# RMS norms on one core: where the squares are added and how the root is spread back

## The reference, cut to what matters

```python
def rms_norm(x, w):
    xf = x.astype(F32)
    y = xf * lax.rsqrt(jnp.mean(xf * xf, -1, keepdims=True) + NORM_EPS) * w.astype(F32)
    return y.astype(x.dtype)

def block(x, mods, nw, fw_in, fw_out, mixer, params, init_state):
    sh1, sc1, g1, sh2, sc2, g2 = mods
    h = rms_norm(x, nw[0]) * (1 + sc1) + sh1
    out, state = mixer(h, init_state, *params)
    x = x + g1 * out
    h = rms_norm(x, nw[1]) * (1 + sc2) + sh2
    x = x + g2 * swiglu(h, fw_in, fw_out)
    return x, state
```

## Time and profile before

| what | value |
|---|---|
| runs of the kernel | 2957.46, 2961.81, 2971.84 us (median 2961.81) |
| the profiled execution: its time | 2957.81 us |
| the profiled execution: its span | 2956.0 us |
| mean granted TensorE clock | 0.903 of full speed |
| TensorE matmul / weight load busy | 2465.6 / 2249.1 us (83% / 76%) |
| VectorE / ScalarE busy | 1293.3 / 903.4 us (44% / 31%) |

### The profile page before, as it was taken

How to read it: one execution, slowest core, us unless ns; L and a number is a source line. 1 busy time by engine, 2 the same in 40 slices (tenths; PEclk the granted TensorE clock), 3 DMA queues, 4 the chain that set the end, 5 groups by cost and what they waited for, 6 DMA issues and landing times.

```text
span 2956.0 us, 51987 instructions
## 1 busy us (share of the span) xinstructions
PE 2465.6 (83%) x21424; PEld 2249.1 (76%) x21424; DVE 1293.3 (44%) x2212; ACT 903.4 (31%) x1697; POOL 0.2 (0%) x4
## 2 busy tenths in 40 slices
PE   4799579649996669999797699999985869999797
PEld 2799366238884459999797598888864869999796
DVE  1311644375565442222322477878874232221323
ACT  1322222213331132222212356555553132221311
POOL 0000000000000000000000000000000000000000
PEclk8899678569998789999899799999987989999898
DMA  5122424210001212222122133333330212222121
GB/s 199 50 72 77 142 72 171 92 32 7 3 3 58 78 40 67 76 73 76 52 70 96 39 100 98 94 98 97 93 111 22 64 36 71 78 71 76 54 70 49
DMA packets 319412, 216.46 MB, mean 73 GB/s; under 512 B 11640, under 2 KB 304902, under 8 KB 318854
## 3 DMA queue, kind: packets, MB, share of 16 engines
q1 hardware_dynamic: 260944, 179.66, 20.3%
q10 hardware_dynamic: 58294, 34.41, 3.9%
HBM read 205.74 MB, written 8.29 MB: 72 GB/s over the span
## 4 chain that ended last, share of the span: by engine, by line
PE 75%; DVE 18%; ACT 2%; issue 2%; DMA 1%; DVEq 1%; ACTq 1%; SPq 0%
PE bank L271 46%; PE bank L2022 10%; PE bank L494 2%; PE bank L1279 2%; DVE wide_low L289 1%; PE bank L2057 1%; DVE arena L1492 1%; ACT arena L487 1%; PE bank L412 1%; PE bank L1364 1%; PE bank L2061 1%; DMA ring<-in_mod_w_dram 1%; DVE ring_low L2111 1%; DVE rstd L505 1%; PE bank L1382 1%
## 5 line engine op out<-in xcount | busy, mean ns | idle before, releaser
L271 PE MATMUL bank<-narrow_high,w_split 128*128 128x320 f32 x4096 | 774.0, 311 | 80.9 <-DVE w_split L279 80.9
L271 PEld LDWEIGHTS bank<-narrow_high,w_split 128*128 128x128 f32 x4096 | 648.1, 189 | 81.9 <-issue 81.9
L279 DVE TENSOR_TENSOR w_split<-ring,w_split 128x1024 fp32r<-128x1024 f32 (+1 forms) x192 | 229.4, 1202 | 597.3 <-ACT w_split L276 588.4
L271 PE MATMUL bank<-narrow_low,w_split 128*128 128x320 f32 x2048 | 469.7, 311 | 0.0
L271 PE MATMUL bank<-wide_high,w_split 128*128 128x320 f32 x1920 | 371.3, 316 | 85.5 <-DVE w_split L279 85.5
L276 ACT ACTIVATE w_split<-ring 128x1024 fp32r<-128x1024 f32 (+1 forms) x192 | 198.9, 1042 | 754.5 <-PE bank L271 408.7
L271 PEld LDWEIGHTS bank<-wide_high,w_split 128*128 128x128 f32 x1920 | 310.5, 193 | 87.5 <-issue 87.5
L271 PEld LDWEIGHTS bank<-narrow_low,w_split 128*128 128x128 f32 x2048 | 345.7, 189 | 0.0
L271 PE MATMUL bank<-wide_low,w_split 128*128 128x320 f32 x960 | 223.9, 315 | 0.0
L2022 PE MATMUL bank<-x_high,pair_high 128*128 128x320 f32 x768 | 186.7, 325 | 30.0 <-DVE ring_low L2111 29.9
L1679 DVE TENSOR_TENSOR arena<-arena,bank 128x640 f32 (+1 forms) x44 | 36.1, 821 | 366.8 <-PE bank L271 366.8
(11 more groups left out here) (353 smaller groups left out, 2994.6 us busy)
## 6 DMA issues: line engine op xcount, KB each, us to landing
ring<-in_mod_w_dram SPq DMA_DIRECT2D x96, 512.0 KB, 4.7
ring<-in_ffn_w_in_dram SPq DMA_DIRECT2D x88, 512.0 KB, 3.8
ring<-in_od_w_in_dram SPq DMA_DIRECT2D x48, 512.0 KB, 4.1
arena<-cumulative_decays ACTq DMA_DIRECT2D x80, 256.0 KB, 3.5
ring<-in_ev_w_in_dram SPq DMA_DIRECT2D x32, 512.0 KB, 3.8
ring<-in_ffn_w_out_dram SPq DMA_DIRECT2D x32, 512.0 KB, 3.6
ring<-in_od_w_out_dram SPq DMA_DIRECT2D x16, 512.0 KB, 3.7
ring<-in_ffn_w_out_dram SPq DMA_DIRECT2D x16, 384.0 KB, 3.3
```

The lines of the kernel that those rows point to most:

```text
L271: mm = E.matmul(twin[pr][:, b, :], w_split[:, ws, w, k, :], r(k)[:, b * HT:(b + 1) * HT], start=st and n == 0, stop=en and n == 2)
L279: return V.tensor_tensor(w_split[:, ws, 1, 0:kt], ring[:, s, 0:kt], w_split[:, ws, 0, 0:kt].bitcast(F32), ALU.subtract)
```

## The change

ACT's squares stay. Instead of 8 (or 16) tiles of products on PE, DVE adds the tiles of squares elementwise into `rstd` (128x640), 7 (or 15) additions, each waiting for the one before and for its square. Then PE takes five products, each with one 128x128 chunk of that sum as the stationary operand and a single column of ones moving, so that the sums over partitions land as five columns, with the 128 tokens of a chunk on the partitions (`bank[:, 4, 0:5]`). Scale and epsilon, root and reciprocal run on those 128x5 elements, in `small[:, 11:16]`. To bring the result back to tokens along the free dimension, DVE multiplies the identity by each column (five diagonal 128x128 matrices, in `rstd`), and PE multiplies ones by each diagonal, which spreads it over all partitions into `pair[0]` in PSUM. The scaling of lines 509 and 512 reads it there, no longer from SBUF. In n4 square k now waits for the addition of tile k-2. The diff:

```diff
--- before.py
+++ after.py
@@ -460,13 +460,18 @@
         return vec[:, v:v + n]
 
 
-    norm_sems = [sem(f"norm_{n}") for n in ("squares", "sum", "mean", "root", "scaled")]
+    norm_sems = [sem(f"norm_{n}") for n in ("squares", "added", "sum", "mean", "root", "scaled", "diagonal",
+                                                 "spread")]
     norm_tiles, norm_turns = [0], [0]
 
     def stage_norm(src, dst, kt, scale_at, weight, shift_at, name):
 
-        sq_s, ss_s, m_s, rt_s, h_s = norm_sems
+
+
+        sq_s, ad_s, ss_s, m_s, rt_s, h_s, dg_s, sp_s = norm_sems
+        sums, root, spread = bank[:, 4, 0:NCH], small[:, 11:16], pair[0][:, 0:T]
         t0, n0 = norm_tiles[0], norm_turns[0]
+        a0 = t0 - n0
         norm_tiles[0] += kt
         norm_turns[0] += 1
         sq = dst if kt == KD else take(2, T)
@@ -475,11 +480,10 @@
         def act(act):
             for k in range(kt):
                 if ring2 and k >= 2:
-                    act.wait_ge(ss_s, t0 + k - 1)
+                    act.wait_ge(ad_s, a0 + max(k - 2, 1))
                 A.activation(sq[:, k % 2 if ring2 else k, :], src[:, k, :], ACT.Square).then_inc(sq_s, 1)
             act.wait_ge(m_s, n0 + 1)
-            la.done(A.activation(rstd[:, :], rstd[:, :], ACT.Sqrt))
-            act.sem_inc(rt_s, 1)
+            A.activation(root, root, ACT.Sqrt).then_inc(rt_s, 1)
             if shift_at is not None:
                 for k in range(kt):
                     act.wait_ge(h_s, t0 + k + 1)
@@ -488,28 +492,39 @@
                                      bias=mod[:, shift_at + k, s:s + 1])
 
         def pe(pe):
-            for k in range(kt):
-                pe.wait_ge(sq_s, t0 + k + 1)
-                q = sq[:, k % 2 if ring2 else k, :]
-                E.matmul(pairs[2][:, LAT], ones, q[:, LAT], start=(k == 0), stop=(k == kt - 1))
-                E.matmul(pairs[2][:, CTX], ones, q[:, CTX], start=(k == 0), stop=(k == kt - 1)).then_inc(ss_s, 1)
+            pe.wait_ge(ad_s, a0 + kt - 1)
+            for c in range(NCH):
+                mm = E.matmul(sums[:, c:c + 1], rstd[:, chunk(c)], ones[:, 0:1], start=True, stop=True)
+            mm.then_inc(ss_s, 1)
+            for c in range(NCH):
+                pe.wait_ge(dg_s, n0 * NCH + c + 1)
+                mm = E.matmul(spread[:, chunk(c)], ones, rstd[:, chunk(c)], start=True, stop=True)
+            mm.then_inc(sp_s, 1)
 
         def dve(dve):
             if scale_at is not None:
                 lv.done(V.scalar_tensor_tensor(amp[:, :, :], mod[:, scale_at:scale_at + KD, :], 1.0,
                                                weight.unsqueeze(2).to_broadcast([P, KD, 2]), ALU.add, ALU.mult))
-            dve.wait_ge(ss_s, t0 + kt)
-            lv.done(V.tensor_scalar(rstd[:, :], pairs[2][:, 0:T], 1.0 / (kt * P), EPS, ALU.mult, ALU.add))
-            dve.sem_inc(m_s, 1)
+            for k in range(1, kt):
+                dve.wait_ge(sq_s, t0 + k + 1)
+                if k > 1:
+                    dve.wait_ge(ad_s, a0 + k - 1)
+                V.tensor_tensor(rstd[:, :], sq[:, 0, :] if k == 1 else rstd[:, :], sq[:, k % 2 if ring2 else k, :],
+                                ALU.add).then_inc(ad_s, 1)
+            dve.wait_ge(ss_s, n0 + 1)
+            V.tensor_scalar(root, sums, 1.0 / (kt * P), EPS, ALU.mult, ALU.add).then_inc(m_s, 1)
             dve.wait_ge(rt_s, n0 + 1)
-            lv.done(V.reciprocal(rstd[:, :], rstd[:, :]))
+            lv.done(V.reciprocal(root, root))
+            for c in range(NCH):
+                V.tensor_scalar(rstd[:, chunk(c)], ident, root[:, c:c + 1], None, ALU.mult).then_inc(dg_s, 1)
+            dve.wait_ge(sp_s, n0 + 1)
             for k in range(kt):
                 if scale_at is not None:
                     for s, c in ((1, LAT), (0, CTX)):
-                        ins = V.scalar_tensor_tensor(dst[:, k, c], src[:, k, c], amp[:, k, s:s + 1], rstd[:, c],
+                        ins = V.scalar_tensor_tensor(dst[:, k, c], src[:, k, c], amp[:, k, s:s + 1], spread[:, c],
                                                      ALU.mult, ALU.mult)
                 else:
-                    ins = V.scalar_tensor_tensor(dst[:, k, :], src[:, k, :], weight[:, k:k + 1], rstd[:, :],
+                    ins = V.scalar_tensor_tensor(dst[:, k, :], src[:, k, :], weight[:, k:k + 1], spread,
                                                  ALU.mult, ALU.mult)
                 ins.then_inc(h_s, 1)
 
```

## The result

| | before | changed |
|---|---|---|
| median of 7 runs | 2963.88 us | 2937.64 us |
| lowest, highest | 2954.82, 2971.84 | 2932.04, 2949.57 |
| profiled execution: time, span | 2957.81, 2956.0 | 2934.3, 2932.5 |
| mean granted TensorE clock | 0.903 | 0.896 |

The ratio of changed to before is 0.9919, with a 95% interval of 0.9896 to 0.9941. That is 24 us faster, at 2937.6 us, where 2937 had been forecast.

A forecast was written before the change was run, and what follows sets the result against it. Six norm turns between fences, 111.6 us from first square to first scaling, were taken as on the path. Five at 13.6 plus 21.4 make 89.4, 22.2 us less: 2935.6, put at 2937 us; eight-in-ten range 2924 to 2954.

The forecast's parts named there:

- n4: The norm turn with 16 tiles, 26.22 us before; forecast at 21.4 us from first square to first scaling.
- half-way step: Runs' median stood 4.0 us above the profiled execution; the forecast was put between, at 2937 instead of 2935.6 us.
- The rivals' times: TensorE clock high 2924 (chance 0.10), dearer PSUM reads 2942 (0.08), exposed loads 2953 (0.12), half-rate PSUM operand 2973 us (0.03).
- Additions: Seven chained VectorE additions in a turn of 8 tiles, 0.855 us each, ending 7.37 us after the first square.
- upper bound of the prediction: 0.93 us for one VectorE addition, taking the 0.11 us hand-over between engines in place of the 0.035 gap.
- First burst: Five one-column TensorE products after the additions, loads 0.43 us apart at the lower clock: 2.35 us.
- loads exposed: Rival: TensorE products spaced 0.72 instead of 0.43 us, saving only 4.8 us, about 2953 us; chance 0.12.
- Mean, root, reciprocal: Three small operations on 128x5 after the first five products: 0.84 us with hand-overs, against 5.7 us before.
- Second burst: Five spreading products on TensorE, 128 moving columns, 0.43 us each; burst about 2.4 us, diagonals staying ahead.
- Clock: TensorE's product bursts in the norm turns assumed at the lower level (1.2 GHz) after idling through squares and additions.
- clock high: Rival: TensorE keeps or regains its upper clock in the turns, saving 35 us, about 2924 us; chance 0.10.
- Scaling from PSUM: Lines 509 and 512 read an operand from PSUM: costed at nothing; the skill's figures would add 5.7 us.

The follow-up runs named there:

- one_wait: Changed kernel, but in turns of 8 tiles additions 3, 5 and 7 wait only for the addition before; 2939.8 us, 0.9945 of the kernel before.
- warm: Changed kernel plus unused 512-column products on TensorE while ScalarE squares and VectorE adds; 2937.5 us, 0.9931 of the kernel before.
- adds_alone: Changed kernel, but two products by ones sum and spread at once, then mean, root and reciprocal run on 128x640; 2941.3 us, 0.9957 of the kernel before.
- pe_columns: Changed kernel without VectorE additions: TensorE takes each tile's squares as stationary operand, five one-column products per tile; 2986.3 us, 1.0100 of the kernel before.

## Why the prediction was right, point by point

- *Total.* 2937 was forecast, 2937.6 measured. Part of that agreement is luck. The turns gave 20.3 us where the sum had 22.2. The two profiled spans differ by 2956.0 - 2932.5 = 23.5 us, so 3.2 us lie in the stages between the turns, which the sum had at nothing; the largest part is 2.3 us between n4's first scaling and f1's first square (157.3 and 154.9 us), a stretch that scatters from 153.7 to 157.6 us over the versions. And the half-way step between the profiled execution and the median of before was worth 1.4 us. The rivals' times carry that step in part (2924 and 2942) and in part not (2953 and 2973), which decides nothing.
- *Additions.* The term that was mis-sized: 0.93 us instead of 0.855, and the seventh ended 7.86 us after the first square, not 7.37. The sum took a chain's gap from instructions with a single wait (0.035 us); here two waits stand before each, and one_wait showed 0.86 with one and 0.93 with two. The upper bound of the prediction, 0.93, had been argued from another cause and happened to be the value.
- *First burst.* 2.35 forecast, 63.76 + 2.26 - 63.73 = 2.29 measured. The spacing of lines 844 to 846 held down to a single column, and "loads exposed" fell.
- *Mean, root, reciprocal.* 0.84 forecast; 66.69 - 66.02 = 0.67 measured, with hand-overs of 0.03 to 0.04 us in place of 0.07 to 0.11. The instruction times (163, 208, 189 ns) were within 15 ns of those taken from the earlier trace rows. From the last addition to the first scaling 5.99 us instead of 6.21, which pays back half of what the additions lost.
- *Second burst.* 2.50 with all five products, 2.36 forecast; the diagonals stayed ahead.
- *Clock.* The changed kernel's bursts ran at the lower level in all six turns, as assumed; f1 lost its lucky start, and that too was in the sum. One reading of the kernel before was wrong, without weight in the sum: n1 and f0 started at the lower level, but n3, n4 and n5 did not. In these three the granted clock was 1.00 at the first product and fell 1.3 to 1.5 us after the first square (first two instructions 1.64, 1.43 and 1.66 us, n1's 2.05). That the lower clock is what makes the bursts long was only argued then; warm shows it (1.17 and 1.38 us). The 13 us that the "clock high" rival set on it are 9.9 where unused products brought most of it back.
- *Scaling from PSUM.* No cost. The rule cited from the Trainium skill (Perfetto Trace Analysis, "Optimizing Scalar/DVE Operations"), 65 ns more for an instruction on PSUM, doesn't show: 743 against 747 and 343 against 346 ns.
- *n4.* 22.02 against 21.4 forecast: the additions, spaced 0.93 us instead of 0.86, ended 0.9 us later than in the sum, and the shorter tail gave 0.2 back.

## What to carry to other kernels

Where an operation with a long price for each column (here a reciprocal at 4.15 us for 640 columns) runs over data that hold the same value in all 128 partitions, turn the data first: five one-column products, three operations of 0.2 us, five diagonals and five products to spread it back took 6.0 us, where adds_alone needs 16.45 - 7.86 = 8.6 for the same, and three quarters of the gain (15.9 of 20.3 us) came from there, with the sum moved to VectorE first. Count the waits before each link of a dependent chain, since the second one costs about 70 ns there and nothing that shows off the chain. And price the bursts that follow a long idle stretch of TensorE at its lower clock: here the first burst of each turn came after more than 8 us without a product, and all twelve ran at 0.50.

## What the runs showed that I had not expected

TensorE stayed at 1.2 GHz for all but the first half microsecond of 34 us (n4 in pe_columns), with float32 weight loads and one-column products running without a pause. Under the 512-column products of the kernel before the clock had risen 3.9 to 4.9 us after the first square in all turns but f1, where it was up from the start. A busy row of PE and PEld is no sign of the upper clock; the granted clock has to be read.

Two profiled executions of the same changed kernel agree within 0.01 us in every turn, and in the sum of the turns, but their spans are 2932.5 and 2940.5 us. The difference lies in stages that the change doesn't touch: from the end of n1's turn to f0's first square 998.9 and 1002.7 us, from the end of n3's turn to n4's first square 589.6 and 593.3 us. In both stretches the longer one has the lower granted clock, 0.844 against 0.847 and 0.939 against 0.946, and length times clock is the same to 0.2%. So the two executions differ by what the clock of the untouched stages does, and effects of a few microseconds are read here from the turns and not from the medians. What moves that clock is not settled.

adds_alone goes beyond that. By its turns it should be at 0.9985 of the kernel before, and its ten runs put it at 0.9957, with an interval (0.9939 to 0.9976) that excludes this. In its profiled execution the stretch from the end of n3's turn to n4's first square takes 580.5 us where the kernel before has 589.9, at 0.950 against 0.941. Its clock accounts for some 5 of the 9.4 us. So the runs alone would have put the additions at 13 us and not at 4.4, and why that stage was shorter stays open.
